# One order of products instead of two phases in a weight-split matrix multiply of a hybrid decoder layer

## The reference, cut to what matters

```python
def layer_tail(x, mix, w_out, g_mlp, w_up, w_down, g_ple, w_ple, w_ple_gate, p):
    x = x + mix @ w_out
    x = x + jnp.square(jax.nn.relu(rmsnorm(x, g_mlp) @ w_up)) @ w_down
    x = x + (p @ w_ple) * jax.nn.sigmoid(rmsnorm(x, g_ple) @ w_ple_gate)
    return x
```

## Time and profile before

| | |
|---|---|
| median of 3 runs | 1929.42 us (1929.1 to 1929.66) |
| the profiled execution, its own time | 1929.1 us |
| its span | 1927.3 us |
| PE busy | 1842.0 us, 96% of the span |
| PEld, DVE, ACT, POOL busy | 89%, 47%, 34%, 31% |
| chain that ended last: PE | 61% of the span |
| of that, lines 206 and 210 (`multiply`) | 25% and 13% |

### The profile page before, as it was taken

How to read it: one execution, slowest core, us unless ns; L and a number is a source line. 1 busy time by engine, 2 the same in 40 slices (tenths; PEclk the granted TensorE clock), 3 DMA queues, 4 the chain that set the end, 5 groups by cost and what they waited for, 6 DMA issues and landing times.

```text
span 1927.3 us, 35068 instructions
## 1 busy us (share of the span) xinstructions
PE 1842.0 (96%) x13394; PEld 1720.7 (89%) x13394; DVE 912.7 (47%) x1622; ACT 660.8 (34%) x1231; POOL 597.6 (31%) x599
## 2 busy tenths in 40 slices
PE   7999978999996999999999999999999999999998
PEld 6999977999994766676899999999999999999898
DVE  4699954766447666767523221222122222124425
ACT  4312213345325665656423221111112121214335
POOL 0002881423205434343353222222222222225531
PEclk8999998999998999999999999999999999999999
DMA  5322364555413343443313111111111111112114
GB/s 159 91 60 61 78 177 125 142 122 138 127 46 110 117 125 116 129 121 101 113 55 129 50 34 55 39 50 40 55 45 44 45 44 55 39 45 94 48 40 134
DMA packets 194380, 163.66 MB, mean 85 GB/s; under 512 B 23109, under 2 KB 177426, under 8 KB 193568
## 3 DMA queue, kind: packets, MB, share of 16 engines
q1 hardware_dynamic: 175421, 138.06, 24.4%
q0 software_dynamic: 5952, 16.26, 3.2%
q10 hardware_dynamic: 12842, 7.09, 1.4%
HBM read 147.70 MB, written 18.25 MB: 86 GB/s over the span
## 4 chain that ended last, share of the span: by engine, by line
PE 61%; DVE 3%; ACT 3%; POOL 2%; issue 2%; POOLq 0%; DVEq 0%; ACTq 0%
PE ps L206 25%; PE ps L210 13%; PE ps L2219 5%; PE ps L2591 4%; PE ps L1675 3%; PE ps L1652 3%; PE ps L1663 3%; PE ps L1702 2%; DVE S L1919 1%; ACT S L1802 1%; PE ps L2608 1%; PE ps L1710 1%; PE ps L1738 1%; PE ps L1719 0%; POOL S L1619 0%
## 5 line engine op out<-in xcount | busy, mean ns | idle before, releaser
L192 POOL TENSOR_TENSOR wm_lo<-wm_raw,wm_hi 128x512 fp32r<-128x512 f32 (+1 forms) x96 | 169.3, 1764 | 546.9 <-ACT wm_hi L187 546.9
L2408 DVE TENSOR_TENSOR xT<-ps,xT 128x1056 f32<-128x1056 f32 x64 | 80.5, 1258 | 254.7 <-PE ps L210 254.7
L1619 POOL TENSOR_SCALAR S<-S,inv,gate_p 128x64 f32<-128x64 f32 (+6 forms) x192 | 122.6, 656 | 203.3 <-DVE inv L1929 203.3
L936 PE MATMUL ps_p<-Xhi,w1hi 128*128 128x256 f32 x544 | 160.3, 295 | 10.7 <-ACT Xhi L666 10.7
L187 ACT ACTIVATE wm_hi<-wm_raw 128x512 fp32r<-128x512 f32 (+1 forms) x96 | 73.9, 770 | 281.3 <-PE ps L210 281.3
L206 PE MATMUL ps<-Ahi,wm_hi 128*128 128x352 f32 x768 | 165.6, 323 | 1.8 <-ACT wm_hi L187 1.2
L206 PE MATMUL ps<-Hhi,wm_hi 128*128 128x352 f32 x768 | 165.5, 323 | 0.0
L206 PE MATMUL ps<-Alo,wm_hi 128*128 128x352 f32 x768 | 164.6, 322 | 0.0
L206 PE MATMUL ps<-Hlo,wm_hi 128*128 128x352 f32 x768 | 164.6, 322 | 0.0
L1066 DVE SCALAR_TENSOR_TENSOR y<-u,conv_w,y 128x1024 f32<-128x1024 f32 x120 | 155.5, 1341 | 1.2
L936 PE MATMUL ps_p<-Xhi,w1lo 128*128 128x256 f32 x544 | 154.4, 284 | 0.0
(11 more groups left out here) (380 smaller groups left out, 3958.1 us busy)
## 6 DMA issues: line engine op xcount, KB each, us to landing
s_raw<-in_cache_slc_kv_dram SPq DMA_DIRECT2D x256, 128.0 KB, 2.1
raw<-in_cache_cmp_kv_dram SPq DMA_DIRECT2D x132, 128.0 KB, 4.3
wm_raw<-in_w_up_dram SPq DMA_DIRECT2D x32, 512.0 KB, 4.0
wm_raw<-in_w_down_dram SPq DMA_DIRECT2D x64, 256.0 KB, 2.6
raw<-in_cache_cmp_kv_dram POOLq DMA_DIRECT2D x124, 128.0 KB, 4.7
win_raw<-in_w_in_dram SPq DMA_DIRECT2D x38, 256.0 KB, 3.4
wg_raw<-in_w_ple_gate_dram SPq DMA_DIRECT2D x14, 512.0 KB, 3.7
xT<-x_spill SPq DMA_DIRECT2D x2, 2112.0 KB, 11.2
```

Source lines behind the costliest of these rows:

```text
L192: self.c.nc.gpsimd.tensor_tensor(self.lo[s][:, 0:nk, :], self.raw[s % self.raw_slots][:, 0:nk, :], self.hi[s][:, 0:nk, :].bitcast(F32), AL ...
L936: mm = nc.tensor.matmul(ps_h[n % 2][:, 0:w], ws[cc][:, j, :], x[n % 2][:, j % 8, slice(j // 8, j // 8 + w)], start=(j == 0 and m == 0), st ...
L1619: nc.gpsimd.tensor_scalar(x, x, inv[:, n % 3, 3 * e + br:3 * e + br + 1], c.gate_p[:, i, H * br + h:H * br + h + 1], ALU.mult, ALU.mult).t ...
L2408: nc.vector.tensor_tensor(three(x), banks[s][:, :, 0:CH], three(x), ALU.add).then_inc(W.free, 1)
```

## The change

`multiply` now waits for `lo_ready` of its tile at its head, where it waited for `hi_ready` (GpSimd raises `lo_ready` only after it has seen `hi_ready`, so the high part is there too). Inside each block k it issues the three products in turn; before, it went through all blocks with the two products of the high weights, then waited for `lo_ready`, and went through all blocks again with the low weights.

```diff
         nk = nk or self.nk
-        after(pe, self.hi_ready, t + 1)
+        after(pe, self.lo_ready, t + 1)
         after(pe, self.free, t - 1)
         nc = self.c.nc
         for k in range(nk):
             if before is not None:
                 before(k)
-            for n, x in enumerate((xhi, xlo)):
+            for n, (w, x) in enumerate(((self.hi, xhi), (self.hi, xlo), (self.lo, xhi))):
                 for j in range(NCH):
-                    nc.tensor.matmul(ps[:, j, 0:CH], self.hi[s][:, k, :], x(k)[:, CH * j:CH * j + CH], start=(k == 0 and n == 0), stop=False)
-        after(pe, self.lo_ready, t + 1)
-        for k in range(nk):
-            for j in range(NCH):
-                mm = nc.tensor.matmul(ps[:, j, 0:CH], self.lo[s][:, k, :], xhi(k)[:, CH * j:CH * j + CH], start=False, stop=(k == nk - 1))
+                    mm = nc.tensor.matmul(ps[:, j, 0:CH], w[s][:, k, :], x(k)[:, CH * j:CH * j + CH],
+                                          start=(k == 0 and n == 0), stop=(k == nk - 1 and n == 2))
         mm.then_inc(self.done, 1)
```

## The result

| | before | changed |
|---|---|---|
| median | 1929.54 us (4 runs, 1929.10 to 1931.09) | 1941.94 us (4 runs, 1937.95 to 1942.74) |
| ratio | | 1.0058, 95% interval 1.0041 to 1.0077 |
| again, in a later comparison | 1930.93 us (21 runs, 1924.02 to 1935.78) | 1940.28 us (5 runs, 1939.19 to 1941.31) |
| ratio | | 1.0045, 95% interval 1.0031 to 1.0059 |
| span of the profiled execution | 1927.3 us | 1941.8 us |

The change makes the kernel slower, as forecast, but by 9 to 12 us and not by 8.4. Both medians lie above the range (up to 1939.9).

What follows compares the result with a forecast made beforehand. TensorE was taken to carry the chain. Tile 2 1.08, up tiles 2.01, down tiles 1.94 and seven waits 3.36 summed to 8.4 us, giving 1937.8 us, 0.43% more; range 1933.6 to 1939.9 us.

Steps and rivals of the forecast that it cites:

- The pace: MLP tiles: the new order slows up tiles from 11.587 to 11.653 us and down tiles by 0.034 to 5.827.
- The first rival: MLP tiles: the order costs nothing, the 0.067 us belongs to two other stages; 4.4 us, 1933.8 us; chance 0.12.
- The seven waits: Second down tile behind up tiles, seven times: waits for GpSimd's low part, 0.48 us each, 3.36 us together.
- The second rival: Second down tiles: low part comes 0.4 us earlier, so no waits show; 5.3 us, 1934.7 us; chance 0.07.
- the fourth: All 96 tiles: a head wait holds back weight loads, 0.09 us each, 8.6 us on top, 1946.4 us; chance 0.05.
- Tile 0 and tile 2: Tile 0 loses its 1.7 us stall, but later sums make tile 2 wait 2.6 us and stand 1.08 us later.
- Rival 3: Tile 2: tile 0 keeps its gain, price -1.7 us; with both no-cost rivals too, 1927.7 us; chance 0.02.

Runs made afterwards that it cites:

- bank_outer: Kernel before, but tiles 1 to 95 go through one PSUM bank after the other and wait for the low part at the head; timed once, 1936.3 us.
- wait_alone: Kernel before with its old order of products, but each tile waits for its low part at its head; 1934.21 us, ratio 1.0015.
- tile0_alone: Kernel before, but tile 0 alone takes the three products in turn, with the head waiting for the high part; ratio 1.0002.
- sums_late: Kernel before with the norm's sums moved in tile 0: first two at k = 7, third behind the last high product; 1930.46 us, ratio 0.9995.
- tile0_wait: Kernel before, but tile 0 alone takes the three products in turn and every tile waits for its low part at its head; 1938.15 us, ratio 1.0035.
- sums_early: Changed kernel with the norm's sums one block earlier in tile 0 (k = 4 and k = 6); 1941.14 us, ratio 1.0053.

## Why the prediction was wrong, point by point

**The pace.** Forecast 11.653 and 5.827 us a tile, measured the same in the changed kernel and in the kernel with the order alone. The sum of it, 4.0 us, stands. The first rival (order costs nothing) is refuted for these orders, and with it the result that the prediction drew from the formula of the Trainium skill ("TensorE: Matmul & The Clock Gate", "Back-to-back issue gap"). That section gives the formula for an isolated matmul; of a stream in which each matmul has its own weight load, as here, it says that both set the spacing. The order of operands has no place in either. That a pace belongs to an order for good, as the prediction took it, is true of the changed kernel and not of `bank_outer`.

**The seven waits.** Forecast 0.48 us each with the tile ahead. Measured: tiles 8 and 9 take 6.18 + 5.89 = 12.07 us instead of 11.59, less 0.03 for tile 9's own pace: 0.45, seven times 3.1 us against 3.4. With the old order (`wait_alone`) the seven waits give 3.45. The second rival is refuted, and so is the fourth: in `wait_alone` every tile waits at its head and all but those behind the waits keep their pace.

**Tile 0 and tile 2.** Forecast: tile 0 gains 1.7, the third sum is 1.66 later, a wait of 2.6 us, tile 2 stands 1.08 us later. Measured: 15.14 - 13.41 = 1.73, 1.66, 2.45 us, and 0.95 plus 0.09 for the restart. Rival 3, that the gain stays, is refuted for the changed kernel; with the wait for the low part put off in tile 2 the gain does stay (`tile0_alone`).

**The step that failed** is "it waits 2.6 us, starts at 1062.19, and with the restart stands as if it had begun at 1062.28". The price of the wait was taken from restarts at full clock (0.09 us) and went no further: the sum put the lower clock at nothing. In all three profiles with a wait of about 2.5 us at tile 2 (2.45, 2.4, 2.51) the granted clock fell to the lower level, between 0.2 us before the restart and 1.2 us after it, and stayed there for 3.4 us, which cost 13.24 - 11.74 = 1.5 us; in those with 1.02 and 1.35 us, and in those without a wait there, it did not fall. The profile of the kernel before could have warned of it. Behind the MLP it has two waits of TensorE for GpSimd's low part, 2.23 us up to 1786.49 (the place of the earlier trace rows) and 2.21 us up to 1809.63. Behind the first, from which the lag was read, the clock stayed up; behind the second it fell:

```profile
1787.00:1791.00 4.00, 4.00 (x25) 4.00 (x24) 2.27 (x4) 4.00 (x4) 3.12 (x1) 1.00 0.44 131
...
1809.00:1813.00 4.00, 3.37 (x11) 3.37 (x12) 1.39 (x1) 2.57 (x3) 2.04 (x2) 0.57 0.44 131
```

The slices of the earlier trace rows are too coarse to show 3.4 us of it, and I used that row only to compare stages.

Forecast 8.4 plus 1.5 is 9.9; the MLP grew by 9.25 and 9.29, the rest being 0.03 a wait and some tenths at the turns of the loop, and the second comparison of the runs shows 9.35. The times alone would not tell 8.4 from 9.3: the interval of that comparison is 6.0 to 11.4 us.

**What is left of the first comparison.** There the medians lie 12.4 us apart, 3 us more than the MLP explains. In the profiled pair the start of the MLP is 1.4 us later and the part behind it 3.8 us longer; both have stretches at the lower clock that the kernel before did not have in its profile. The windows of the changed kernel:

```profile
937.00:947.00 10.00, 7.76 (x39) 7.25 (x36) 8.21 (x7) 1.41 (x3) 0.64 (x1) 0.66 0.57 216
1797.00:1803.00 6.00, 5.81 (x24) 5.82 (x25) 4.25 (x4) 6.00 (x5) 4.53 (x3) 0.72 0.30 87
1821.00:1828.00 7.00, 6.10 (x26) 6.11 (x27) 1.66 (x1) 2.62 (x3) 4.68 (x3) 0.76 0.25 75
```

and of the kernel before:

```profile
937.00:947.00 10.00, 7.54 (x60) 7.13 (x61) 9.34 (x8) 2.53 (x4) 1.78 (x1) 1.00 0.44 159
```

The change has no instruction ahead of the MLP, so the first cannot be its doing. The later ones stand at three waits of TensorE that all fourteen profiles have, those of the kernel before and of `sums_late` too: the two of 2.2 us above and one of 2.5 us near the end. By the granted clock in fine windows, it fell at the first of them in 5 of the 14 profiles, at the second in 5 and at the third in 9, each time between 0.5 us before the restart and 1.5 us after it; the profile of the kernel before has one of the three, the first one of the changed kernel all three, its second one two. In the MLP, on the other hand, none of the 31 idle times of 0.7 to 1.5 us was followed by the lower clock. So a wait of over 2 us makes the fall possible, not certain, and three of three at tile 2 do not show that it comes there in every execution.

Such stretches come and go in executions of one and the same kernel: in 69 later runs of the kernel before, the time ran from 1924.0 to 1937.0 us, and was longer where the mean granted clock was lower (0.979 to 0.986; correlation -0.90, about 1.3 us for each 0.001). So four runs a side were too few for a few us: the interval of the first comparison is 7.9 to 14.9 us. Whether the part behind the MLP is slower more often after the change (3.8 and 2.3 us longer in its two profiles, 2.2 in `tile0_wait`, 0.0 to 1.7 us in the others, -1.5 in `sums_early`) is not settled; the same waits in every kernel speak for chance.

**The range** was therefore too narrow on the upper side: it held nothing for the clock, and the scatter of the kernel before had been judged from three runs within 0.6 us.

## What to carry to other kernels

Before moving a wait to the head of a tile, go through all tiles and compare the end of what is waited for with the tile's start; the few that are late, not the average slack, carry the price, and a stall filled in one place may come back where the work behind it is due. Where the new wait is long, put what the lower clock costs behind it (here 1.5 us) into the range: it came behind 22 of 45 waits of 2.2 to 2.5 us, and behind none of 0.7 to 1.5 us in the MLP. Look for such waits in fine windows of the profile before. Keep a wait directly ahead of the first instruction that reads the data: here that alone saves the seven waits, and with the clock effect about 5 us of 9.3.

## What the runs showed of the hardware that was not expected

Matmuls of the same size, all with their own weight load, ran at different steady paces in different orders: 11.587 us for 72 when the two input parts alternate on six matmuls of one weight slice, 11.640 with one part at a time, 11.653 with the three products in turn; which of the two input parts comes first makes no difference. With one bank at a time, one and the same instructions ran at 11.640 and at 11.480, and changed from one to the other at restarts behind waits of 0.3 to 0.4 us. At tile 2 a wait of 2.5 us of TensorE cost 1.5 us more behind it by the granted clock; at other waits of 2.2 to 2.5 us the clock fell in some executions and not in others.
